# Routing weights of a peer layer by one weighted product per token, and turns between stages by column halves with the first weight splits on GpSimd

## The reference

```python
def peer_ffn(h, w_q, sub_keys, peer_u, peer_v):        # for blocks of 128 tokens
    q = einsum('td,de->te', xb, w_q).reshape(128, 8, 2, 128)
    s = einsum('thpk,pnk->thpn', q, sub_keys)            # 128 keys in each half
    s_top, i_top = top_k(s, 16)
    ...                                                  # 16 best pairs per head
    g = softmax(g_top)
    act = gelu(einsum('thkd,td->thk', peer_u[expert], xb))
    return einsum('thk,thkd->td', g * act, peer_v[expert])
```

## Time and profile before

| | |
|---|---|
| time, median of 3 runs | 2693.94 us (2690.03 to 2698.76) |
| profiled execution, span from first to last instruction | 2688.2 us |
| busy: TensorE, VectorE, ScalarE, GpSimd | 97%, 74%, 56%, 13% |
| mean granted TensorE clock | 0.995 of full |
| HBM | 182 GB/s over the span |

### The profile page before, as it was taken

How to read it: one execution, slowest core, us unless ns; L and a number is a source line. 1 busy time by engine, 2 the same in 40 slices (tenths; PEclk the granted TensorE clock), 3 DMA queues, 4 the chain that set the end, 5 groups by cost and what they waited for, 6 DMA issues and landing times.

```text
span 2688.2 us, 48883 instructions
## 1 busy us (share of the span) xinstructions
PE 2605.5 (97%) x17304; PEld 2387.0 (89%) x17304; DVE 1996.2 (74%) x3791; ACT 1506.0 (56%) x2602; POOL 346.1 (13%) x190
## 2 busy tenths in 40 slices
PE   6999999999999999999999999999999999998998
PEld 6779999999888888889999999888888889887997
DVE  6768957888887876669867888666666686677766
ACT  4455557766565556555557766665554544463443
POOL 4007600000000002617500000000000101002000
PEclk9999999999999999999999999999999999999999
DMA  6844564444788874424664444555555345442553
GB/s 243 282 137 164 197 228 149 142 143 148 266 279 272 280 264 145 149 94 167 204 213 143 148 142 150 195 191 192 195 187 187 108 176 188 165 164 96 187 188 133
DMA packets 134733, 490.88 MB, mean 183 GB/s; under 512 B 15520, under 2 KB 15608, under 8 KB 134288
## 3 DMA queue, kind: packets, MB, share of 16 engines
q1 hardware_dynamic: 131904, 480.31, 52.6%
q0 software_dynamic: 2640, 8.02, 0.9%
HBM read 487.21 MB, written 1.06 MB: 182 GB/s over the span
## 4 chain that ended last, share of the span: by engine, by line
PE 87%; DVE 6%; ACT 2%; DMA 2%; issue 1%; POOL 0%; SPq 0%; DVEq 0%; ACTq 0%
PE ps L224 78%; PE ps L1308 4%; DMA weight_ring<-in_stream 2%; ACT weight_split L239 1%; PE ps L641 1%; DVE weight_split L248 1%; DVE arena L633 1%; ACT arena L396 1%; PE ps L2473 1%; PE ps L1280 1%; POOL weight_split L248 0%; DVE arena L1909 0%; PE ps L389 0%; DVE arena L1913 0%; PE ps L662 0%
## 5 line engine op out<-in xcount | busy, mean ns | idle before, releaser
L224 PE MATMUL ps<-hT_split,weight_split 128*128 128x256 f32 x9792 | 1234.3, 285 | 9.8 <-DVE hT_split L421 4.6
L224 PEld LDWEIGHTS ps<-hT_split,weight_split 128*128 128x128 f32 x9792 | 1196.2, 192 | 20.1 <-issue 13.8
L248 DVE TENSOR_TENSOR weight_split<-weight_ring,weight_split 128x1024 fp32r<-128x1024 f32 x674 | 823.5, 1223 | 403.0 <-ACT weight_split L239 400.4
L239 ACT ACTIVATE weight_split<-weight_ring 128x1024 fp32r<-128x1024 f32 x800 | 848.2, 1061 | 259.7 <-PE ps L224 167.8
L224 PE MATMUL ps<-weight_split,hidden_split 128*128 128x512 f32 x3948 | 914.8, 391 | 7.6 <-DVE hidden_split L1574 4.0
L224 PEld LDWEIGHTS ps<-weight_split,hidden_split 128*128 128x128 f32 x3948 | 736.4, 188 | 160.9 <-issue 8.0
L248 POOL TENSOR_TENSOR weight_split<-weight_ring,weight_split 128x1024 fp32r<-128x1024 f32 x126 | 306.2, 2433 | 410.5 <-ACT weight_split L239 410.2
L1404 ACT ACTIVATE hidden_split<-arena 128x256 fp32r<-128x256 f32 (+1 forms) x256 | 176.3, 689 | 249.0 <-PE ps L224 248.5
L1396 ACT ACTIVATE arena<-ps 128x256 f32<-128x256 f32 (+18 forms) x248 | 126.9, 512 | 133.5 <-PE ps L224 133.5
L224 PE MATMUL ps<-weight_split,hT_split 128*128 128x512 f32 x660 | 159.1, 396 | 9.0 <-DVE weight_split L248 4.7
L1574 DVE TENSOR_TENSOR hidden_split<-arena,hidden_split 128x256 fp32r<-128x256 f32 x256 | 161.2, 630 | 0.0
(11 more groups left out here) (357 smaller groups left out, 1765.7 us busy)
## 6 DMA issues: line engine op xcount, KB each, us to landing
weight_ring<-in_stream SPq DMA_DIRECT2D x912, 512.0 KB, 3.3
x<-in_x SPq DMA_DIRECT2D x1, 1024.0 KB, 5.0
arena<-mlstm_m_rows POOLq DMA_DIRECT2D x1, 1024.0 KB, 6.7
arena<-in_ln_mix_g POOLq DMA_DIRECT2D x2, 512.0 KB, 4.8
arena<-in_ln_mix_b POOLq DMA_DIRECT2D x2, 512.0 KB, 6.2
arena<-in_ln_ffn_g POOLq DMA_DIRECT2D x2, 512.0 KB, 4.6
arena<-in_ln_ffn_b POOLq DMA_DIRECT2D x2, 512.0 KB, 6.3
out<-x SPq DMA_DIRECT2D x2, 512.0 KB, 2.6
```

The lines of the kernel that those rows point to most:

```text
L224: mm = pe.matmul(out_, stationary(s_part), moving(m_part), start=start and n == 0, stop=stop and n == 2, skip_group_check=True)
L239: act.activation(wsplit[:, n % SPLITS, HIGH, :], ring[:, slot(POS[n]), :], ACT.Copy).then_inc(high_ready, 1)
L248: eng.tensor_tensor(w[:, REST, :], ring[:, slot(POS[n]), :], w[:, HIGH, :].bitcast(fp32), ALU.subtract).then_inc(split_ready, 1)
```

## The change

**Routing.** `pr_gain` holds g in two parts, high in fp32r and the rest. The operand over i becomes a plain one-hot, made on GpSimd. The operand over j becomes a pair: g high at column j and g rest at column j, 256 columns, made on VectorE by one scalar_tensor_tensor per token (`places_j`, two tokens in each call). TensorE makes one fp32r product of 128 x 256 per token; a step takes two PSUM banks. ScalarE copies the high half to SBUF (`high_out`), VectorE adds the rest half to it (`summed`), into `pr_w` for the tiles that have been and into place for the later ones. GpSimd does `weigh` from `pr_w`. ScalarE's share of the one-hots and `keep` go.

**Turns.** The second half of the tokens is taken by column halves: its products for columns 0 to 511 come first (`third_done`), and x, the norm, the transposes and the splits follow in five parts (`OUT_PARTS`). The variance steps on VectorE go into the bias of ScalarE's roots. The first two column tiles of a stage are multiplied in turns by chunks 0 to 3 and 4 to 7 (`two_lin_cols`). The rest of a stage's first tile, and high (in rms turns) and rest of the second, are on GpSimd (`first_rests_pool`, `layer_norm_pool`), ahead of its parameter DMAs; in layer norm turns GpSimd also does the unit scaling of the first half. The holds are fewer. The dense stages end on three tiles by halves where it was two.

```diff
+                tile(5, 1).then_inc(tiles_used, 1)
+                tile(6, 1, (0,))
+                tile(7, 1, (0,)).then_inc(third_done, 1)
+                tile(6, 1, (1,)).then_inc(tiles_used, 1)
+                tile(7, 1, (1,)).then_inc(tiles_used, 1)
...
+        def two_lin_cols(n, dsts, turn):
+
+            for chunks in (range(4), range(4, 8)):
+                for k, dst in enumerate(dsts):
+                    if chunks[0] == 0:
+                        pe.wait_ge(split_ready, n + k + 1)
+                    w = wsplit[:, (n + k) % SPLITS]
+                    for c in chunks:
+                        if k == 0:
+                            chunk_split(turn, c)
+                        mm = passes(dst, lambda part: w[:, part, c * 128:(c + 1) * 128], lambda part: hTsplit[:, part, c, :], c == 0, c == 7)
+                    if chunks[0]:
+                        mm.then_inc(tiles_used, 1)
...
-        HOLDS = {1: (28, 2, 4, 14, 2), 2: (28, 5, 4, 14, 0), 4: (28, 5, 4, 14, 0), 6: (0, 1, 26, 14, 1),
-                 7: (0, 7, 26, 14, 0), 8: (0, 6, 26, 14, 0)}
...
+        HOLDS = {1: (14, 2, 2, 12, 2), 2: (14, 5, 2, 12, 0), 4: (14, 5, 2, 12, 0), 6: (0, 1, 8, 10, 1),
+                 7: (0, 7, 8, 10, 0), 8: (0, 6, 8, 10, 0)}
...
+        def part_split_dve(n, part, of, normed):
+
+            high, low = (of(hTsplit[:, k]) for k in (HIGH, REST))
+            dve.wait_ge(turned_out, OUT_BASE[n] + part)
+            after_dve(dve.tensor_copy(high, of(normed)))
+            dve.tensor_tensor(low, of(normed), high.bitcast(fp32), ALU.subtract).then_inc(x_split_ready, 1)
+
+        def norm_turn_dve(n, normed):
+
+            part_split_dve(n, 1, lambda v: half_of(v, 0), normed)
             for m in range(2):
-                high, low = (pair_of(hTsplit[:, k], m) for k in (HIGH, REST))
-                dve.wait_ge(turned_out, 4 * n + 3 + m)
-                after_dve(dve.tensor_copy(high, pair_of(normed, m)))
-                dve.tensor_tensor(low, pair_of(normed, m), high.bitcast(fp32), ALU.subtract).then_inc(x_split_ready, 1)
...
+            high(n0)
+            act.wait_ge(x_half, k)
+            square(0, 0, slice(0, D))
+            root(0, 1, 0, rms_eps)
+            act.wait_ge(x_third, k)
+            square(1, 1, slice(0, 512))
+            act.wait_ge(x_ready, k)
+            square(1, 2, slice(512, D))
+            act.wait_ge(rms_bias, k)
+            root(1, 3, 2, second_bias)
+
+        def rms_bias_dve(k):
...
+        def residual_dve(k, gate_k, gate, done_tiles, rms=None, bank=0):
+
+            def gated_sum(tb, columns, done):
+                y = ps[:, bank + 2 * tb:bank + 2 * tb + 2, :].rearrange("p a b -> p (a b)")
+                after_dve(dve.tensor_tensor(tok[:, tb, columns], y[:, columns], gate[:, columns], ALU.mult))
+                dve.tensor_tensor(x[:, tb, columns], x[:, tb, columns], tok[:, tb, columns], ALU.add).then_inc(done, 1)
+
+            dve.wait_ge(half_done, k + 1)
             dve.wait_ge(gate_ready, gate_k + 1)
-            after_dve(gated_dve(0, gate, bank))
-            add_dve(0)
-            splits_until(dve, n0)
-            rest(dve, n0)
-            rows_done(k, 1, done_tiles)
-            after_dve(gated_dve(1, gate, bank))
+            gated_sum(0, slice(0, D), x_half)
+            dve.wait_ge(third_done, k + 1)
+            gated_sum(1, slice(0, 512), x_third)
+            dve.wait_ge(tiles_used, done_tiles)
+            gated_sum(1, slice(512, D), x_ready)
...
+        def layer_norm_pool(k, n0):
+
+            pool.wait_ge(ln_rstd, k + 1)
+            ln_unit(pool, 0, 0).then_inc(unit_first, 1)
+            ln_unit(pool, 0, 1).then_inc(x_half, 1)
+            splits_until(pool, n0)
+            rest(pool, n0)
+            rest(pool, n0 + 1)
...
+        def first_rests_pool(n0):
+
+            splits_until(pool, n0)
+            rest(pool, n0)
+            pool.wait_ge(tiles_used, n0 + 1 - SPLITS + 1)
+            pool.wait_ge(tile_full[slot(POS[n0 + 1])], full(POS[n0 + 1]))
+            pool.tensor_copy(wsplit[:, (n0 + 1) % SPLITS, HIGH, :], ring[:, slot(POS[n0 + 1]), :]).then_inc(high_ready, 1)
+            rest(pool, n0 + 1)
+
...
-        def step_weights(q):
-            return ps[:, q % 3, :].rearrange("p (a j) -> p a j", a=STEP)
+        def step_weights(q, part):
+
+            b = 2 * (q % 2)
+            return ps[:, b:b + 2, :].rearrange("p b (a k j) -> p (b a) k j", a=2, k=2)[:, :, part, :]
...
+            def places_i(q):
+                if q >= 2:
+                    pool.wait_ge(pr_built, STEPS * l + q - 1)
+                for a in range(STEP):
+                    step = pool.tensor_scalar(pr_ohi[:, q % 2, a], iota[:], pr_cols[:, 0, STEP * q + a:STEP * q + a + 1], None, ALU.is_equal)
+                step.then_inc(pr_ohi_r, 1)
+
+            def weigh(q):
+
+                w, tokens = pr_w[:, q % 2], slice(STEP * q, STEP * q + STEP)
+                pool.wait_ge(pr_summed, STEPS * l + q + 1)
+                pool.wait_ge(activated_ready, 128 * l + STEP_AT[q])
+                early, late = acts_early[:, tokens, :], acts_late[:, tokens, 0:STEP_AT[q] - EARLY]
+                pool.tensor_tensor(early, early, w[:, :, 0:EARLY], ALU.mult)
+                pool.tensor_tensor(late, late, w[:, :, EARLY:STEP_AT[q]], ALU.mult).then_inc(pr_routed, 1)
+
+            pool.wait_ge(pr_cols_out, 2 * (l + 1))
+            pool.wait_ge(mod_ready, 14 if l else 6)
+            places_i(0)
+            places_i(1)
+            for q in range(STEPS):
+                weigh(q)
+                if q + 2 < STEPS:
+                    places_i(q + 2)
 
         def peer_pe(l, turn):
...
-                pe.wait_ge(pr_ohj_act, STEPS * l + q + 1)
-                pe.wait_ge(pr_ohj_dve, STEPS * l + q + 1)
-                if q >= 3:
-
-                    pe.wait_ge(pr_routed, STEPS * l + q - 2)
-                    pe.wait_ge(pr_kept, STEPS * l + q - 2)
+                pe.wait_ge(pr_ohj_r, 2 * (STEPS * l + q + 1))
+                if q >= 2:
+
+                    pe.wait_ge(pr_summed, STEPS * l + q - 1)
                 for a in range(STEP):
-                    mm = pe.matmul(ps[:, q % 3, 128 * a:128 * a + 128], pr_ohi[:, q % 2, a, :], pr_ohj[:, q % 3, a, :].bitcast(fp32),
-                                   start=True, stop=True)
+                    mm = pe.matmul(ps[:, 2 * (q % 2) + a // 2, 256 * (a % 2):256 * (a % 2) + 256], pr_ohi[:, q % 2, a, :],
+                                   pr_ohj[:, (STEP * q + a) % J_SLOTS].rearrange("p k j -> p (k j)"), start=True, stop=True)
...
-            def keep(q):
-
-                act.wait_ge(pr_routed, STEPS * l + q + 1)
-                act.activation(acts_late[:, STEP * q:STEP * q + STEP, STEP_AT[q] - EARLY:], step_weights(q)[:, :, STEP_AT[q]:], ACT.Copy).then_inc(pr_kept, 1)
-
-            def places_j(q):
-                if q >= 3:
-                    act.wait_ge(pr_built, STEPS * l + q - 2)
-                for a in range(ACT_J):
-                    step = act.activation(pr_ohj[:, q % 3, a, :], iota[:], ACT.Abs, scale=-1.0, bias=pr_cols[:, 1, STEP * q + a:STEP * q + a + 1])
-                step.then_inc(pr_distance, 1)
-                act.wait_ge(pr_distance, STEPS * l + q + 1)
-                near = pr_ohj[:, q % 3, 0:ACT_J]
-                act.activation(near, near.bitcast(fp32), ACT.Relu, scale=-1.0, bias=1.0).then_inc(pr_ohj_act, 1)
+            def high_out(q):
+
+                act.wait_ge(pr_built, STEPS * l + q + 1)
+                if q >= 2:
+                    act.wait_ge(pr_routed, STEPS * l + q - 1)
+                    act.wait_ge(pr_kept, STEPS * l + q - 1)
+                act.activation(pr_w[:, q % 2], step_weights(q, HIGH), ACT.Copy).then_inc(pr_high_out, 1)
 
...
-            def weigh(q):
-
-                g, tokens = step_weights(q), slice(STEP * q, STEP * q + STEP)
-                dve.wait_ge(pr_built, STEPS * l + q + 1)
-                dve.wait_ge(activated_ready, 128 * l + STEP_AT[q])
-                early, late = acts_early[:, tokens, :], acts_late[:, tokens, 0:STEP_AT[q] - EARLY]
-                dve.tensor_tensor(early, early, g[:, :, 0:EARLY], ALU.mult)
-                dve.tensor_tensor(late, late, g[:, :, EARLY:STEP_AT[q]], ALU.mult).then_inc(pr_routed, 1)
+            def gains_rest():
+                dve.wait_ge(pr_cols_out, 2 * (l + 1))
+                dve.tensor_tensor(pr_gain[:, REST, :], ps[:, 3, 0:T], pr_gain[:, HIGH, :].bitcast(fp32), ALU.subtract).then_inc(pr_gain_r, 1)
+                dve.wait_ge(pr_gain_r, l + 1)
+
+            def summed(q):
+
+                w, low, tokens = pr_w[:, q % 2], step_weights(q, REST), slice(STEP * q, STEP * q + STEP)
+                dve.wait_ge(pr_high_out, STEPS * l + q + 1)
+                dve.tensor_tensor(w[:, :, 0:STEP_AT[q]], low[:, :, 0:STEP_AT[q]], w[:, :, 0:STEP_AT[q]], ALU.add).then_inc(pr_summed, 1)
```

(21 more changed lines are left out.)

372 lines of the change are left out of this document (194 added, 178 removed).

## The result

The changed kernel takes 2809.64 us (median of four executions, 2802.35 to 2813.07) against 2691.99 us of the kernel before, a ratio of 1.0439 with an interval of 1.0418 to 1.0459. The prediction was 2712 us with a range of 2645 to 2775: the direction was right, the size was not. In the table further down, one of the eight executions of old_turns_shared, 4108 us at a granted clock of 0.57, is left out of the median; the profiled one was this one, so no trace of that kernel is read.

The account below looks back on a forecast made before the run. TensorE was taken to bound the kernel (97% busy, 87% of the chain). The profiled span of 2688.2 plus 16 for routing, 2.5 for turns and 5.7 around the span gave 2712 us; range 2645 to 2775.

Parts of the forecast that it names:

- The forecast's 16 us: Routing: VectorE held off by GpSimd makes a period 30.1 us instead of 29.2, 16 us lost over 18.3 periods.
- TensorE's step of 0.48 us, period of 26.4: Routing: four fp32r products of 0.12 us make a step; eight tiles with seven steps fall from 29.20 to 26.4 us.
- GpSimd's own step is 2.6 us, so it isn't the bound: Routing: GpSimd's two weighs (0.65, 0.53) and four places_i of 0.35 us sum to 2.6 us a step.
- Rival 3: Routing: GpSimd's short instructions are dear, 0.28 us of hold or more; 2767 us, more if GpSimd becomes the chain; chance 0.20.
- the bound from the two-input rate: Routing: upper bound of 0.28 us for a places_i's hold on VectorE, against 0.11 from GpSimd's fill; 0.15 was taken.
- The port, c = 0.5 us on VectorE: Routing: taking turns with GpSimd over SBUF inputs adds 0.5 us to VectorE's step, 4.1 us instead of 3.6.
- VectorE's 3.6 us a step: Routing: VectorE's step without meetings: one-hots 1.55, two additions 0.68, weight rest 1.14, weigh_tile 0.22 us.
- the 48 us worked out for a routing without meetings: Routing: gain if VectorE were never held off, 18.3 periods falling from 29.2 to 26.6 us.
- The turns, +2.5 us: Stage turns: +0.5 us for each of three rms turns, 0 for layer norm and hybrid turns, 1 for a clock fall.
- The weaving: Turns: a stage's first two tiles woven by halves, with the finer waits, give 1 us back in an rms turn.
- The peer stages' DMAs, 0: Peer turns: parameter DMAs behind GpSimd's splits land by 192.9 us, ahead of the first product at 193.5; cost nothing.
- What would show it: Signs in the routing stage and turns that would mark the forecast right or wrong, such as periods of about 30 us.

Follow-up runs that it names:

- old_turns_shared: Changed kernel with two of four GpSimd one-hots on ScalarE, VectorE's one-hots reading the row from PSUM, and the turns of the kernel before: 2682.38 us.
- mended_order: both_mended with one of eight routing weight splits on GpSimd, and GpSimd's one-hots of step q+2 made before the weigh of step q: 2658.38 us.
- turns_only: The changed kernel with the routing functions of the kernel before: +12.1 us over the kernel before.
- both_mended: Changed kernel, two of four GpSimd one-hots on ScalarE, VectorE's one-hots reading PSUM, and GpSimd taken out of the turns by column halves: 2682.78 us.
- turns_no_pool: turns_only with the first splits and the first half's normalising taken off GpSimd, onto VectorE and ScalarE: 2690.72 us.
- one_subtract_psum: Changed kernel, GpSimd's four comparisons a step made one subtraction (other weights computed), VectorE's one-hots reading the row from PSUM: 2706.33 us.
- after_order: The changed kernel with GpSimd's one-hots of step q+2 queued before the weigh of step q, nothing else: 32 us less than the changed kernel.

## Why the prediction was right or wrong

- **Slower, as forecast, but not by the mechanism.** The forecast's 16 us were VectorE held off by GpSimd; what the trace shows is TensorE waiting for GpSimd's one-hots. That the sign came out right was in part luck.
- **TensorE's step of 0.48 us, period of 26.4: right.** mended_order's first period is 26.4 us.
- **"GpSimd's own step is 2.6 us, so it isn't the bound": this is the step that failed.** The term is places_i at 0.35 us (0.2 to start, 0.15 of hold, taken near the fill of the earlier trace rows "as it reads one tensor"). Alone it takes 0.58 to 0.59 us, and 0.93 in the mean. With 0.58 alone the same sum gives 0.54 + 0.51 + 4 x 0.58 = 3.4 us; with the meetings it is 4.8, and the period 35 us. Rival 3 named this, place and threshold ("from 0.7 us a places_i"), gave 2767 us "and more", and had a chance of 0.20. A memset reads nothing and was no neighbour of an operation with a number per partition; the bound from the two-input rate (0.28 of hold, 0.48 in all) was no bound either, since the form with one tensor is the dearer one.
- **The port, c = 0.5 us on VectorE: right that it is dear, wrong in who pays.** VectorE lost 4 x (0.554 - 0.477) = 0.31 us a step on the one-hots and 0.06 on the weight rest (1.28 us in the mean of the stage, 1.22 in turns_only), near the 0.37 at which the prediction saw routing break even; GpSimd lost 4 x (0.929 - 0.590) = 1.36. The sum had charged GpSimd nothing for meetings, though the earlier trace rows show both sides waiting.
- **VectorE's 3.6 us a step: too small, hidden by the rest.** The one-hots were well sized (0.39 each; four in 1.65 with the tail). The two additions take 0.84 (594.62 to 595.46), not 0.68, and weigh_tile 0.43 in mid-stage, not the 0.22 of an early step: a cost that grows along the stage was read at its start. With the port free both_mended runs at 4.0 us a step there. Even the best version, mended_order, gives less than the 48 us worked out for a routing without meetings: its stage is 14.7 us shorter per layer, 29 in all.
- **The turns, +2.5 us: 12 were measured.** In the first turn the working was nearly right as far as it went: it had the halves of tok ready at 189.4 and 190.5, and in turns_only, whose old stage ends 1.0 us later, they are at 190.91 and 191.89. But the price put on it was 0.5 and the turn is 2.5 longer to the first product. The weaving gave 0.3 back, not 1: from there to the end of the second tile it is 6.00 us where it was 6.31. The copy takes 1.50 us, not 1.0. For a layer norm turn the prediction said 0; such turns cost 1.8, 0.4 and 0.7. GpSimd's normalising takes 2.07 us for 512 elements there where VectorE takes 0.54; how much of the cost is this and how much its splits, no run separates.
- **The peer stages' DMAs, 0: right.** In turns_only they are issued from 190.11 on and in by 194.14, and the first product comes at 196.29.
- **What would show it**: of the signs named, the additions above 0.7 us (2.12) were right. VectorE's one-hots (0.55 against 0.47) and the weight rest (1.28 against 1.22 in that stage) went the way named, but by less than "well above". The periods of 30 us, VectorE near full and TensorE waiting for VectorE's one-hots were not right; "places_i over 0.5 us with GpSimd full" is what came.

The turns named add up to 9 of the 12 us: 2.5, 2.0 (the turn into the stick-breaking attention, by its first transposes), 1.8, 1.8, 0.4 and 0.7. The profiled execution of turns_only spans 14.4 us more than the one of before, and its trace shows where most of the rest lies. Ahead of the first turn it is 1.0 us late; the last product there ends anywhere from 180.8 to 187.7 us in the profiled executions, with no edit ahead of it that explains that. The clock is part of it: ahead of that product the kernel before had 10.2 us at half the full clock, the changed kernel 23.9. In the turn into the hybrid stage, for which the prediction had 0, the first 72 products took 11.44 us where they took 8.87, in turns_only and then in the kernel before:

```profile
2036.48 11.44 PE L232 MATMUL ps<-hT_split,weight_split 128*128 128x256 f32 x72 [1.07 <-DVE hT_split L393]
```

```profile
2029.48 8.87 PE L224 MATMUL ps<-hT_split,weight_split 128*128 128x256 f32 x72 [1.07 <-DVE hT_split L368]
```

From 2035.5 to 2042.3 the granted clock was 0.50 there, 1.2 GHz, and 1.00 in the stretch of before (2025 to 2042). TensorE had stood for 2.03 us for VectorE just ahead of it, where it had stood for 1.70 before. That is the fall which the prediction's +1 allowed for, and 2.6 us of it in this execution; turns_no_pool has it too, for half as long (3.4 us from 2027.6). Whether the fewer holds brought it about, no run tests.

## What to carry to other kernels

Work moved to an idle engine has to be priced by a row of its own form on that engine, start, operand kinds and all; if there is none, the bound must reach to where that engine becomes the chain. Where two engines share a port, charge a meeting to both, and look first for an operand that can live in PSUM: it gave 70 us here with no work removed. And when a faster engine brings nothing, look in the queues for an instruction that stands behind another which waits: swapping two calls gave 8 us, and 16 more to an edit that had been worth nothing.

## What the runs showed of the hardware

- GpSimd's comparison of a tensor with a number per partition takes 590 ns at 128 elements; its subtraction and product with two such numbers takes 2059 to 2084 ns at 512, about 4 ns an element. Its operation on two tensors takes 0.35 us at 80 columns, 0.58 at 204, 1.04 at 512 (one_subtract_psum) and 2.34 at the least at 1024, 2.43 in the mean: 2.1 ns an element from 204 to 1024, an estimate from these two. The Trainium skill (GPSIMD Engine Reference, 4.1 Engine selection) calls two-input work about half as fast as VectorE's and one-input work roughly line-rate. The first agrees (2.43 against 1.22 us at 1024); the second is contradicted for this form (2.07 us, VectorE 0.54).
- A GpSimd operation on two tensors beside VectorE's one-hots made VectorE the loser (0.72 us mean where it is 0.48 unhindered, GpSimd 1.22 where it is 1.04); GpSimd's short ones with a number per partition lost more themselves (0.93 for 0.59, VectorE 0.55 for 0.48). Why, beyond the order of issue, stays open.
- Waits of up to 1.6 us a step left TensorE's granted clock at 1.00 (the fifth period and later). In the first four periods it stood at 0.91 to 0.95, with five slow tiles a layer, each behind a wait of 1.8 to 3.6 us; one wait of 2.30 us (before 461.81) had no such tile behind it, nor had one of 1.83 in the second layer of after_order. The slow tiles add 6.6 and 6.7 us. How much of that reaches the routing's 106 us was not isolated; after_order, with one such tile in the first layer and none in the second, is 24 us shorter in those periods of the two layers, its shorter waits included.
